# One-core transformer layer step: the closing gate made as rows behind the chosen lists, and one context product put ahead of the first latents

## The reference, cut to what matters

```python
sh_m, sc_m, gt_m, sh_f, sc_f, gt_f = split(silu(c) @ w_mod + b_mod, 6)   # one set each for context and latents
...
h = rms_norm(x, g_pre_ffn) * (1.0 + sc_f) + sh_f
x = x + gt_f * rms_norm(ec_ffn(h, ...), g_post_ffn)
...
aff = softmax(xt @ w_router)
top_v, top_i = top_k(aff.T, cap)          # cap = 2 n / 16: 32 context tokens, 128 latents for each expert
xs = take(xt, top_i)
hid = silu(xs @ w1[e]) * (xs @ w3[e])
out.at[top_i].add((hid @ w2[e]) * top_v)
```

## Time and profile before

| | us |
|---|---|
| median of 3 runs | 2828.32 (2819.99 to 2830.44) |
| the profiled execution, its own time | 2830.08 |
| its span, first to last instruction | 2828.3 |
| PE busy | 2667.8 (94%) |
| DVE busy | 1565.6 (55%) |
| ACT busy | 1193.5 (42%) |
| POOL busy | 239.2 (8%) |

### The profile page before, as it was taken

One profiled execution on the slowest core, in us unless ns is written; L12 is line 12 of the kernel. 1 busy time (PEld: TensorE's weight loads), 2 busy tenths in 40 slices (PEclk: granted clock), 3 DMA queues, 4 the chain that ended last, 5 costly groups with the idle time before them and its releaser, 6 DMA issues.

```text
span 2828.3 us, 36327 instructions
## 1 busy us (share of the span) xinstructions
PE 2667.8 (94%) x14578; PEld 1974.9 (70%) x14578; DVE 1565.6 (55%) x2408; ACT 1193.5 (42%) x1886; POOL 239.2 (8%) x257
## 2 busy tenths in 40 slices
PE   5999799999999999999999999997699999999993
PEld 3444488888788576766767788885477777777772
DVE  1555666666343435454453453555677776777774
ACT  2311444454333313232232333343566666666663
POOL 1111100000000001010100000000011010101012
PEclk9999999999999999999999999998799999999997
DMA  8320000000110010010100110333688888888876
GB/s 288 136 76 30 1 1 0 0 0 0 60 60 16 7 30 23 1 53 1 30 23 31 34 60 30 131 122 136 226 303 292 294 297 297 286 307 289 297 257 203
DMA packets 179023, 334.27 MB, mean 118 GB/s; under 512 B 16468, under 2 KB 40532, under 8 KB 178870
## 3 DMA queue, kind: packets, MB, share of 16 engines
q1 hardware_dynamic: 167172, 303.73, 30.3%
q0 software_dynamic: 9472, 28.32, 3.9%
q10 hardware_dynamic: 2228, 0.11, 0.1%
HBM read 299.12 MB, written 33.03 MB: 117 GB/s over the span
## 4 chain that ended last, share of the span: by engine, by line
PE 65%; issue 20%; DMA 7%; ACT 3%; DVE 3%; POOL 1%; ACTq 0%; POOLq 0%; SPq 0%; DVEq 0%
PE ps L227 16%; PE ps L905 16%; DMA ffn_scratch<-WK 6%; PE ps L743 6%; PE ps L703 5%; PE ps L1677 4%; PE ps L1193 3%; PE ps L728 3%; PE ps L1257 2%; PE ps L1274 1%; PE ps L2191 1%; PE ps L1253 1%; PE ps L349 1%; PE ps L1703 1%; PE ps L1237 1%
## 5 line engine op out<-in xcount | busy, mean ns | idle before, releaser
L227 PE MATMUL ps<-RW,R 128*128 128x256 f32 (+1 forms) x1760 | 503.6, 440 | 0.0
L227 PEld LDWEIGHTS ps<-RW,R 128*128 128x128 f32 x1760 | 327.3, 190 | 141.6 <-issue 112.1
L2267 ACT ACTIVATE RWr<-R 128x1024 fp32r<-128x1024 f32 x384 | 378.0, 1053 | 77.3 <-PE ps L2191 74.4
L2363 DVE TENSOR_TENSOR W_low<-R,RWr 128x1024 fp32r<-128x1024 f32 x256 | 301.8, 1222 | 80.8 <-ACT RWr L2267 80.8
L2191 PE MATMUL ps<-RWr,R1r 128*128 128x512 f32 x1024 | 332.5, 398 | 2.7 <-DVE W_low L2363 1.7
L905 PE MATMUL ps<-W_high,tile_high 128*128 128x512 f32 x640 | 251.3, 393 | 7.3 <-DVE W_low L983 7.3
L905 PE MATMUL ps<-W_low,tile_high 128*128 128x512 f32 x640 | 250.8, 392 | 0.0
L905 PE MATMUL ps<-W_high,tile_low 128*128 128x512 f32 x640 | 250.5, 391 | 0.0
L2191 PEld LDWEIGHTS ps<-RWr,R1r 128*128 128x128 f32 x1024 | 193.0, 189 | 58.8 <-issue 14.6
L975 DVE TENSOR_TENSOR tile_low<-R,tile_high 128x1024 fp32r<-128x1024 f32 x80 | 97.9, 1224 | 164.4 <-ACT tile_high L931 164.2
L2363 DVE TENSOR_TENSOR tile_high<-R,RWr 128x1024 fp32r<-128x1024 f32 x128 | 150.9, 1221 | 31.3 <-ACT RWr L2267 30.9
(11 more groups left out here) (303 smaller groups left out, 4134.4 us busy)
## 6 DMA issues: line engine op xcount, KB each, us to landing
R<-in_w_dram SPq DMA_DIRECT2D x96, 2048.0 KB, 13.5
RW<-in_w_in_dram SPq DMA_DIRECT2D x7, 2048.0 KB, 7.8
R<-in_w_mod_dram SPq DMA_DIRECT2D x5, 2048.0 KB, 12.9
RW<-in_w_mod_dram SPq DMA_DIRECT2D x4, 2048.0 KB, 11.2
RW<-in_w_in_dram SPq DMA_DIRECT2D x8, 1024.0 KB, 7.0
WK<-in_w_mod_dram SPq DMA_DIRECT2D x3, 2048.0 KB, 9.0
xhat_scratch<-WK SPq DMA_DIRECT2D x10, 512.0 KB, 3.8
ffn_scratch<-WK SPq DMA_DIRECT2D x10, 512.0 KB, 5.0
```

What stands on the lines that cost most here:

```text
L227: m = pe.matmul(out, lhs(k), Wslot[slot][:, k, off:off + width], start=(k == 0), stop=(k == KD - 1))
L2267: act.activation(ring_high[n % RING], pair_raw[i][j][:, 2 * q:2 * q + 2, :], ACT.Copy).then_inc(S("weights_high"), 1)
L2363: dve.tensor_tensor(ring_low[n % RING], pair_raw[i][j][:, 2 * q:2 * q + 2, :], ring_high[n % RING].bitcast(F32), ALU.subtract).then_inc(S( ...
```

## The change

- **Gate as rows.** SP loads the bias row and the gain row (`row_b`, `row_g`, each twice, 4 KB each) ahead of the gate's weights. PE adds the bias with one more matmul for each half. DVE multiplies by the gain as it reads the row from PSUM. Four matmuls with a stationary operand of 2 rows (`pick`) spread the rows over 128 partitions, and ACT keeps them in `G2b`. The turn to columns, the 8 + 16 small ACT instructions and the four `pe_bcast` are gone. The column forms of gain and bias, loaded at the start of the kernel, are gone too.
- **Order.** The spreading stands behind the chosen lists on PE. The context's lists are turned first, and DVE writes their columns behind its second round. POOL gathers the context rows and expert 0's latents inside the hole (`pool_topk`; `gather` and `gather_ctx` move out of `pool_moe` unchanged), PE turns the context rows behind the gate's matmuls, and ACT scales all eight blocks.
- **Experts.** Expert 0's first context product is put ahead of the turn of its latents. SP's load of expert 1's first pair now also waits for the split of expert 0's unit (0,1). The counts of kept slots are adapted.

```diff
-                (gv[:, 3, :], g_post_ffn[0].rearrange("(k p) -> p k", p=P)),
-                (bg[:, :], b_mod[0, 5 * D:6 * D].rearrange("(k p) -> p k", p=P)),
                 (keep[:, :], k_keep),
...
+        row_b, row_g = R3[0:2, 9 * D:10 * D], WK[0:2, 9 * D:10 * D]
+        pick = WK[0:2, 8 * D + BLK:8 * D + BLK + 2 * P].rearrange("p (j n) -> p j n", j=2)
+        ROWS_LANDED = 48 + 4 * 16
+
...
         def dve_topk(dve, ch):
             begin(dve, "dve", 8)
+            ch(dve.tensor_copy(topf[0:NE, 0:CAP_CTX], topi[0:NE, 0:CAP_CTX]))
+            dve.sem_inc(S("chosen"), 1)
             for r in range(CAP_LAT // 8):
                 best_eight(dve, ch, 1, r)
-            ch(dve.tensor_copy(topf[0:NE, 0:CAP_CTX], topi[0:NE, 0:CAP_CTX]))
+                if r == 1:
+                    dve.wait_ge(S("chosen_turned"), 1)
+                    for c_ in range(4):
+                        ch(dve.memset(quarter[c_ * CAP_CTX:(c_ + 1) * CAP_CTX, :], float(c_)))
+                    ch(dve.tensor_copy(idx_ctx, bank(1, 4)))
+                    ch(dve.tensor_copy(val_cols, bank(0, NE)))
+                    ch(dve.tensor_scalar(idx_cols, bank(7, NE), 4.0, quarter, ALU.mult, ALU.add))
+                    dve.sem_inc(S("chosen"), 1)
             ch(dve.tensor_copy(topf[:, CAP_CTX:CAP], topi[:, CAP_CTX:CAP]))
 
             ch(dve.tensor_scalar(topf[0:NE, CAP_CTX:CAP], topf[0:NE, CAP_CTX:CAP], float(N_CTX), None, ALU.add))
             ch(dve.tensor_scalar(topf[2 * NE:NE2, CAP_CTX:CAP], topf[2 * NE:NE2, CAP_CTX:CAP], float(N_CTX + HALF), None, ALU.add))
             dve.sem_inc(S("chosen"), 1)
-            dve.wait_ge(S("chosen_turned"), 1)
-            for c_ in range(4):
-                ch(dve.memset(quarter[c_ * CAP_CTX:(c_ + 1) * CAP_CTX, :], float(c_)))
-            ch(dve.tensor_copy(idx_ctx, bank(1, 4)))
-            ch(dve.tensor_copy(val_cols, bank(0, NE)))
+            dve.wait_ge(S("bias_landed"), ROWS_LANDED)
+            for n in range(2):
+                dve.wait_ge(S("mod_row"), NU + n + 1)
+                cols = slice(n * BLK, (n + 1) * BLK)
+                ch(dve.tensor_tensor(grow[:, cols], bank(4 + n, BLK, 2), row_g[:, cols], ALU.mult))
+                dve.sem_inc(S("gates_moved"), 1)
+            dve.wait_ge(S("chosen_turned"), 2)
             ch(dve.tensor_copy(first, bank(2, 2 * NE)))
             dve.wait_ge(S("halves_met"), 2)
 
             other = bank(3, 2 * NE)
             ch(dve.tensor_tensor(greater, first[:, 0:NE], other[:, 0:NE], ALU.is_ge))
-            ch(dve.tensor_tensor(val_lat, first[:, 0:NE], other[:, 0:NE], ALU.max))
             ch(dve.tensor_tensor(apart, first[:, NE:2 * NE], other[:, NE:2 * NE], ALU.subtract))
             ch(dve.tensor_tensor(apart, apart, greater, ALU.mult))
             ch(dve.tensor_tensor(idx_lat, apart, other[:, NE:2 * NE], ALU.add))
-            ch(dve.tensor_scalar(idx_cols, bank(4, NE), 4.0, quarter, ALU.mult, ALU.add))
+            dve.sem_inc(S("chosen"), 1)
+            ch(dve.tensor_tensor(val_lat, first[:, 0:NE], other[:, 0:NE], ALU.max))
             end(dve, "dve")
 
         def pe_topk(pe):
             begin(pe, "pe", 8)
-
-            for n in range(2):
-                s_ = (g2_u + n) % 2
-                pe.wait_ge(w_full[s_], w_ready[g2_u + n])
-                for k in range(KD):
-                    m = pe.matmul(bank(4 + n, BLK, 2), cS[:, k, :], Wslot[s_][:, k, :], start=(k == 0), stop=(k == KD - 1))
-                m.then_inc(S("mod_row"), 1)
-            pe.wait_ge(S("gates_moved"), 4 + 2)
-            for k in range(KD):
-                m = pe.transpose(ps[:, 7 * BANK + 2 * k:7 * BANK + 2 * k + 2], grow[:, k * P:(k + 1) * P], ident[0:2, 0:2])
-            m.then_inc(S("mod_columns"), 1)
-            for n in range(4, 8):
-                pe_bcast(pe, n, 6)
             pe.wait_ge(S("chosen"), 1)
             for q in range(4):
                 rows = slice(q * CAP_CTX, (q + 1) * CAP_CTX)
                 pe.matmul(ps[rows, BANK:BANK + 4], topf[0:NE, 0:CAP_CTX], ident[0:NE, q:NE:4], start=True, stop=True)
                 pe.matmul(ps[rows, 0:NE], topv[0:NE, 0:CAP_CTX], ident[0:NE, 0:NE], start=True, stop=True)
-                pe.matmul(ps[rows, 4 * BANK:4 * BANK + NE], topf[0:NE, 0:CAP_CTX], ident[0:NE, 0:NE], start=True, stop=True)
+                m = pe.matmul(ps[rows, 7 * BANK:7 * BANK + NE], topf[0:NE, 0:CAP_CTX], ident[0:NE, 0:NE], start=True, stop=True)
+            m.then_inc(S("chosen_turned"), 1)
+
+            pe.wait_ge(S("bias_landed"), ROWS_LANDED)
+            for n in range(2):
+                s_ = (g2_u + n) % 2
+                pe.wait_ge(w_full[s_], w_ready[g2_u + n])
+                for k in range(KD):
+                    pe.matmul(bank(4 + n, BLK, 2), cS[:, k, :], Wslot[s_][:, k, :], start=(k == 0), stop=False)
+                pe.matmul(bank(4 + n, BLK, 2), ident[0:2, 0:2], row_b[:, n * BLK:(n + 1) * BLK], start=False, stop=True).then_inc(S("mod_row"), 1)
+            pe.wait_ge(S("chosen"), 2)
+            turn_ctx_slots(pe, 0)
+            pe.wait_ge(S("chosen"), 3)
             for a, src in enumerate((topv, topf)):
-                pe.matmul(ps[:, 5 * BANK + a * NE:5 * BANK + (a + 1) * NE], src[2 * NE:NE2, CAP_CTX:CAP], ident[2 * NE:NE2, 2 * NE:NE2], start=True, stop=True)
+                pe.matmul(ps[:, BANK + a * NE:BANK + (a + 1) * NE], src[2 * NE:NE2, CAP_CTX:CAP], ident[2 * NE:NE2, 2 * NE:NE2], start=True, stop=True)
                 m = pe.matmul(ps[:, 2 * BANK + a * NE:2 * BANK + (a + 1) * NE], src[0:NE, CAP_CTX:CAP], ident[0:NE, 0:NE], start=True, stop=True)
             m.then_inc(S("chosen_turned"), 1)
             pe.wait_ge(S("halves_met"), 1)
             pe.matmul(bank(3, 2 * NE), reverse, second, start=True, stop=True).then_inc(S("halves_met"), 1)
+            pe.wait_ge(S("gates_moved"), 4 + 2)
+            pe.wait_ge(S("slots_kept_act"), 1)
+            for n in range(4):
+                j, h = n // 2, n % 2
+                if n >= 2:
+                    pe.wait_ge(S("rows_kept"), 4 + n - 1)
+                pe.matmul(bank(6 - n % 2), pick[:, j, :], grow[:, h * BLK:(h + 1) * BLK], start=True, stop=True).then_inc(S("rows_spread"), 1)
+            pe.wait_ge(S("chosen"), 4)
             end(pe, "pe")
 
         def act_topk(act, ch):
-
             begin(act, "act", 8)
-            act.wait_ge(S("zero_made"), 1)
-            for n in range(2):
-                act.wait_ge(S("mod_row"), NU + n + 1)
-                act.activation(grow[:, n * BLK:(n + 1) * BLK], bank(4 + n, BLK, 2), ACT.Copy).then_inc(S("gates_moved"), 1)
-            act.wait_ge(S("mod_columns"), 1 + NU + 1)
+            ch(act.activation(reverse, ident[:, ::-1], ACT.Copy))
+            for j in range(2):
+                ch(act.activation(pick[:, j, :], ident[0:2, j:j + 1].broadcast_to([2, P]), ACT.Copy))
+            act.wait_ge(S("slots_turned"), 2)
             for k in range(KD):
-                ch(act.activation(G2[:, k, :], ps[:, 7 * BANK + 2 * k:7 * BANK + 2 * k + 2], ACT.Identity, scale=gv[:, 3, k:k + 1], bias=bg[:, k:k + 1]))
-            for n in range(4, 8):
-                j, k = kind_part(n)
-                for q in range(4):
-                    m = act.activation(colb[:, q, :], zero[:, 0:P], ACT.Identity, bias=G2[:, k + q, j:j + 1])
-                    if q < 3:
-                        ch(m)
-                m.then_inc(S("columns_spread"), 1)
-                act.wait_ge(S("rows_spread"), n + 1)
-                act.activation(G2b[j][:, k * P:(k + 4) * P], bank(6), ACT.Copy).then_inc(S("rows_kept"), 1)
-                act.wait_ge(S("rows_kept"), n + 1)
-            ch(act.activation(reverse, ident[:, ::-1], ACT.Copy))
-            act.wait_ge(S("chosen_turned"), 1)
-            act.activation(second, bank(5, 2 * NE), ACT.Copy).then_inc(S("halves_met"), 1)
+                src = ps[:, 6 * BANK + k * P:6 * BANK + (k + 1) * P].rearrange("p (e c) -> p e c", e=GE)
+                ch(act.activation(xc[:, :, k, :], src, ACT.Identity, scale=A2[:, k, 0:1], bias=modT[:, 24 + k, 0:1]))
+            act.sem_inc(S("slots_kept_act"), 1)
+            act.sem_inc(S("slots_kept_dve"), 1)
+            act.wait_ge(S("chosen_turned"), 2)
+            act.activation(second, bank(1, 2 * NE), ACT.Copy).then_inc(S("halves_met"), 1)
+            for n in range(4):
+                j, h = n // 2, n % 2
+                act.wait_ge(S("rows_spread"), 4 + n + 1)
+                act.activation(G2b[j][:, h * BLK:(h + 1) * BLK], bank(6 - n % 2), ACT.Copy).then_inc(S("rows_kept"), 1)
             end(act, "act")
+
+        def pool_topk(pool, ch):
+            begin(pool, "pool", 8)
+            for t in range(2):
+                pool.wait_ge(S(f"x1_stored{t}"), 32 * (NT // 2))
+            pool.wait_ge(S("chosen"), 2)
+            gather_ctx(pool, 0)
+            pool.wait_ge(S("chosen"), 4)
+            gather(pool, 0)
+            end(pool, "pool")
 
         def sp_topk(sp):
             begin(sp, "sp", 8)
 
```

(31 more changed lines are left out.)

53 lines of the change are left out of this document (23 added, 30 removed).

## The result

The changed kernel took 2806.52 us (median of 11 runs, 2803.77 to 2820.22), the kernel before 2823.71 us on the same chip (11 runs, 2818.26 to 2833.13). The ratio is 0.9945, interval 0.9927 to 0.9963: 0.55% faster, 15.5 us by the ratio (17.2 between the two medians). The forecast was 2820.0, and the range ended at 2812. The profiled execution took 2803.77 us with a span of 2802.0.

What follows compares the result with a forecast made beforehand. PE was taken to bound the kernel from the second expert on. The first unit 4.7 us earlier plus 3.6 for the context product made 8.3 us, off the median 2828.3: 2820.0 us, range 2812 to 2829.

Steps and rivals of the forecast that it cites:

- what starts earlier ends earlier by as much: From the second expert on: PE is always busy at full clock, so an earlier start carries through to the end.
- each later expert takes as long as before: Sign expected in the new trace: no change in the time of any expert after the first.
- for a loss I don't see, in either direction: Remainder outside the forecast and rivals, no place or size given; chance 0.04.
- spreading on PE: Four matmuls behind the lists: 5.5 us taken, 4.65 to 5.5 if the clock rises under them, 6.8 if not.
- ACT's first split: Start of the experts' stage after ACT's last copy: 2013.2 instead of 2016.42, far bounds 2012.3 and 2014.5.
- first unit: Expert 0, after DVE's fourth weight chunk, scaling and split: starts at 2023.3, 4.7 us earlier.
- search to turn, gain: Whole gain, 8.3 us: 4.7 by the earlier first unit, 3.6 by the context product leaving PE's path between units.
- rival 2: Experts' stage: pick fills 2 of 128 rows and may not raise the clock; gain 6.4 us, 2822; chance 0.23.
- just hidden: Latents' gather in the hole: 8.8 us beside SP's transfers costs nothing; at 10.1 about 1 to 1.5 us are lost.
- Rival 3: First unit: PE's new work holds the clock up into the units; gain 10.4 us, 2818; chance 0.12.
- Rival 4: Three units without a pause: the product's 3.6 us return as ring waits; gain 4.7, 2823.6; chance 0.07.
- Rival 5: Context gather held up by SP's backlog, delaying the latents' lists: 6 us slower, 2834; chance 0.04.

Runs made afterwards that it cites:

- b_moved: The kernel before with only its three small tensors (G2, bg, a row of gv) moved behind the large ones: median 2819.06 us, ratio 0.9977.
- a_rows128: The changed kernel with pick and the gate's rows made 128 partitions high, zeros in 126 of them: 2813.32 us, one run.
- a_pool_end: The changed kernel with POOL's stage end put ahead of expert 0's latents' gather instead of behind it: 2819.39 us, one run.
- a_pad: The changed kernel with the dropped 128 bytes filled up again by two unused pads: median 2817.03 us, ratio 0.9983 to the kernel before.
- a_product_back: The changed kernel with expert 0's first context product put back between units (0,1) and (1,0): median 2815.66 us, ratio 0.9966 to the kernel before.
- b_again: The kernel before, unchanged, measured once more: median 2826.07 us, ratio 1.0010 to the kernel before.
- a_again: The changed kernel, unchanged, measured once more: 2814.05 us, ratio 0.9947 to the kernel before.
- a_padW128: The changed kernel with one unused pad of 128 bytes directly ahead of the large work tensors: 2818.81 us, one run.
- a_padW256: The changed kernel with one unused pad of 256 bytes ahead of the large work tensors: 2815.94 us, one run.
- a_best: The changed kernel with the spreading ahead of the latents' lists and expert 0's third weight pair held until its latents landed: 2803.27 us, ratio 0.9908 to before.

## Why the prediction was wrong

**The step that failed** is the sentence in the part on what bounds the kernel, "what starts earlier ends earlier by as much", with its counterpart "each later expert takes as long as before". What the change does to the later experts was a term of 0 in the sum. Of the dropped tensors only the loads and one multiply were counted, at 0. The loads were 0 indeed: the search started at 1955.13 in `b_moved` and at 1955.15 in the changed kernel. But the tensors' place wasn't 0. Without their 128 bytes each matmul of the units is 2 to 4 ns shorter, 6.6 us over 15 experts, and 7.9 us from the first turn to the end. With it the step would have given 2820.0 - 7.9 = 2812.1, the lower end of the range. No rival stood for it; the last 0.04, "for a loss I don't see, in either direction", was all that it had, and 0.87 was given to a change of less than half a per cent.

The number 2820.0 was also built on a median of three runs, 2828.32, and eleven runs gave 2823.71, 4.6 us lower. From there 2823.71 - 14.5 = 2809.2; the last 2.7 us to the measured 2806.52 are left to the runs' spread.

**The hole: the mechanism held, two terms were off.** In us after the search's start:

| step | forecast | measured |
|---|---|---|
| chosen lists ready on DVE | 38.0 | 37.8 |
| latents' numbers written | 41.0 | 40.8 |
| latents' gather issued | 42.0 | 41.1 |
| spreading on PE, us | 5.5 | 7.19 |
| ACT's first split | 46.3 | 48.5 |
| first unit | 56.4 | 59.3 |
| search to turn, gain | 8.3 | 6.6 |

- The spreading was mis-sized, and rival 2 had it right: `pick` fills 2 of 128 rows, and the clock stayed at 0.50 through all of it. `a_rows128`, in one trace, shows that it is the rows. Rival 2 also had the product's start at half clock ("up to 2.1 us more"): it took 5.54 instead of 3.59 us. PE ended last, with the turn at 2010.21; DVE's fourth chunk had ended at 2009.44. That its gain, 6.4 us, is nearly the 6.6 measured is partly luck: it was made up of 2.8 and 3.6, and 1.8 and 4.8 were measured.
- Not foreseen was POOL's stage end. ACT's last copy ended at 2002.79, the stage began at 2003.61. Of the 2.2 us by which the split was late, 1.5 are the spreading (1.7 longer, begun 0.2 sooner) and the rest, 0.5 to 0.7, is POOL (`a_pool_end`). I had counted the gather as "just hidden", at 8.8 us (it took 7.0), and looked only at the turn that reads it; here the stage end of the engine that issued it waited too.
- DVE's two gate products took 1.50 us, above my upper bound of 0.7 each. It cost nothing, as the gather was still issued 0.9 us sooner than forecast.

The first unit is therefore 1.8 us earlier, not 4.7. Behind it 38.40 - 33.60 = 4.8 us are gained: the product's 3.59, some 0.5 from the placement (from first unit to turn `a_pad` takes 34.12) and about 0.7 that are left. Most of it fits the first unit's clock, at half until about 4.4 us into the unit before and 3.3 us into it after, an estimate of 0.5 us. 1.8 + 4.8 = 6.6.

**The other rivals.** Rival 3 fell: the clock, up from 2007.5, was at half from 2014.46 on. Between the product and the unit lay nothing but eight transposes and then 4.25 us of waiting. The rule on transposes from the Trainium skill ("TensorE: Matmul & The Clock Gate", Part 4: PE-mode transpose), on which I had let this rival fall, agrees with this trace and is not proved by it, since PE also stood still. Rival 4 fell: 72 matmuls in 18.17 us without a wait, and `a_product_back` shows that the product's move is worth 3.1 us. Rival 5 fell: the four context gathers landed in 7.7 to 10.2 us beside SP's transfers, and PE waited 9.09 us for DVE's lists, not for rows.

**The 11.8 us ahead of the search** are most likely no part of the change. The profile of the kernel before has seven dips of the clock between 725 and 1805 us (3.4 to 6.9 us each), that of the changed kernel three, and the two repetitions, `b_again` and `a_again`, have seven and three again. By these four traces alone the change could have removed dips. The other traces speak against it. `a_pad` and `a_padW128` both have the new order and the old placement, and start the search at 1955.64 (three dips) and 1963.37 (seven). `a_again` and `a_padW256` both have the new order and the short experts, and start at 1955.43 and 1967.48 (three and seven). `b_moved` has three dips in the old order. And one program differs from run to run as much: the changed kernel's 11 runs lie from 2803.77 to 2820.22, with a mean granted clock of 0.978 or 0.979 in the seven shortest and 0.972 to 0.974 in the four longest; the runs of the kernel before have both levels too. Dips aren't all of it: `a_best` and `a_rows128` have three dips as well and start the search 8.6 and 9.7 us later than the changed kernel, and nearly all of that, 8.5 and 8.8 us, is there when the matmuls of L900 begin (733.95 and 734.21 us instead of 725.41).

The same piece of work (columns as in rows 2), in the kernel before and in the changed one:

```profile
968.00:988.00 20.00, 16.76 (x35) 7.76 (x34) 11.39 (x14) 11.79 (x19) 0.00 (x0) 0.83 0.00 1
```

```profile
964.00:984.00 20.00, 16.76 (x42) 7.62 (x41) 11.92 (x15) 11.20 (x19) 0.00 (x0) 1.00 0.00 1
```

In the first the granted clock falls once, in the second not at all, and PE gets 35 records done where the other gets 42. A mean of 0.83 over 20 us is 6.8 us at half clock, up to 3.4 us of time lost; three and seven dips came in both orders and both placements. They make much of the runs' spread, and they don't drop out of the medians: the changed kernel's were 2806.52 and 2814.05. The ratios to the kernel before on the same chip, 0.9945 and 0.9947, and the lowest runs, least touched by them, give one account: 2818.26 before and 2803.77 after, 14.5 us less, which is 6.6 + 7.9.

**What stays open.** Which of the large tensors has to stand on the multiple of 256 bytes, and why. Matmuls of 512 columns in an earlier stage (L900, 393 ns after, 393 ns with the padding's 64 bytes) don't care; there the DMA engines are nearly idle, here they are at 0.86. That a transfer and PE's reads meet in the memory would fit this, but the last expert, whose second half runs without any transfer, speaks against it as the whole cause. A stretch in it with the DMA engines at 0.00 and one group of the units' matmuls, first the kernel before, then the changed one:

```profile
2758.00:2776.00 18.00, 18.00 (x131) 13.53 (x130) 11.58 (x12) 10.19 (x14) 0.00 (x0) 1.00 0.00 1
L2191 PE MATMUL ps<-W_low,R3r 128*128 128x512 f32 x8 | 3.1, 393 | 0.0
```

```profile
2732.00:2750.00 18.00, 18.00 (x134) 13.72 (x133) 11.57 (x12) 10.71 (x14) 0.00 (x0) 1.00 0.00 1
L2215 PE MATMUL ps<-W_low,R3r 128*128 128x512 f32 x7 | 2.7, 390 | 0.0
```

With no transfer beside them the matmuls with `W_low` still differ by 3 ns; `a_pad` has 393 there and `b_moved` 390. These are few records, but the four traces agree. The groups with `RWr` (from 395 to 401 ns in these stretches) don't show the difference clearly.

## What to carry to other kernels

A dropped or added tensor moves all that stands behind it: before a gain or a loss is put down to a new order, compare the time of one stretch that nobody changed, and run the old kernel with the new layout. A stage ends when the last engine's part ends, and here an engine that had issued a gather counted until the gather had landed. In a hole like this one, matmuls behind a wait of several us are to be priced at half clock (here 7.19 us instead of the 5.5 forecast), and a price at full clock needs a row that shows it. And a repetition of each kernel can't show that a difference is luck when both come out as they did; the mixed versions could.
